# A hybrid decoder block on one core: causal masks added by VectorE, first MLP chunk in products of 512 columns, gate rows ahead of low parts

## What is computed

```python
h = rmsnorm(x, g_mix)
qa, ka, va, cq, ckv, kr, gate_a, gate_b = split(h @ w_in)
# path a: 8 heads of 64, rope on q and k; the one key block of 256 is the query's own, so plain causal attention
s = where(key <= query, q @ k.T * scale, -inf); o_a = softmax(s) @ v
# path b: q and k of 96 = 64 + 32 (rope), v of 64, from low-rank latents; same causal softmax
x = x + (sigmoid(gate_a + b0) * (o_a @ w_o_a) + sigmoid(gate_b + b1) * (o_b @ w_o_b)) @ w_out
u = relu(rmsnorm(x, g_mlp) @ w_ff1)              # 1024 x 4096
x = x + (u * u) @ w_ff2                          # 4096 x 1024
return rmsnorm(x, g_final)
```

## Time and profile before

| | |
|---|---|
| runs | 371.0 us median of 3 (370.7, 371.0, 373.78) |
| the profiled execution's own time | 371.31 us |
| its span, first to last instruction | 369.5 us |
| TensorE busy | 360.6 us, 98% of the span |
| VectorE busy | 281.1 us, 76% |
| ScalarE busy | 229.1 us, 62% |
| granted TensorE clock, mean | 0.99 |
| HBM | 75.44 MB read, 1.05 MB written |

### The profile page before, as it was taken

The page is one execution under the profiler, slowest core; times in us unless marked ns, Lnnn a source line. Parts: engine busy times, 40 slices in busy tenths (PEclk is TensorE's granted clock), DMA queues, the critical chain, the costliest instruction groups (busy, mean ns, idle before and its releaser), DMA issues.

```text
span 369.5 us, 5652 instructions
## 1 busy us (share of the span) xinstructions
PE 360.6 (98%) x2180; PEld 316.7 (86%) x2180; DVE 281.1 (76%) x379; ACT 229.1 (62%) x370; POOL 39.8 (11%) x61
## 2 busy tenths in 40 slices
PE   7999999999999999999999999999999999999993
PEld 6998889877778888888899899999999999999982
DVE  3677973964756757779387779997999899998584
ACT  5696435977576656145274657775877777666424
POOL 1232000000000010000120211101111111220002
PEclk8999999999999999999999999999999999999997
DMA  7999756773332364509346799989999999963003
GB/s 241 321 375 321 272 171 229 226 231 111 118 116 109 115 227 162 180 12 305 140 140 220 183 355 237 285 245 264 266 248 318 265 300 295 303 174 115 0 2 114
DMA packets 43430, 76.79 MB, mean 208 GB/s; under 512 B 1875, under 2 KB 21600, under 8 KB 43152
## 3 DMA queue, kind: packets, MB, share of 16 engines
q1 hardware_dynamic: 39072, 66.59, 53.0%
q0 software_dynamic: 4176, 9.64, 13.2%
q10 hardware_dynamic: 160, 0.27, 0.2%
HBM read 75.44 MB, written 1.05 MB: 207 GB/s over the span
## 4 chain that ended last, share of the span: by engine, by line
PE 96%; DMA 1%; DVE 0%; ACT 0%; POOL 0%; issue 0%; SPq 0%; POOLq 0%; ACTq 0%
PE ps L1345 29%; PE ps L1347 29%; PE ps L1346 29%; PE ps L1352 5%; PE ps L1484 2%; PE ps L1510 2%; DMA xs<-in_x_dram 1%; PE ps L1467 0%; POOL qkT_b L511 0%; PE ps L1423 0%; ACT qkT_b L524 0%; DVE xT_lo L1078 0%; DVE xs L1102 0%; ACT xT_hi L524 0%; POOLq L125 0%
## 5 line engine op out<-in xcount | busy, mean ns | idle before, releaser
L524 ACT ACTIVATE whi<-raw 128x1024 fp32r<-128x1024 f32 (+3 forms) x124 | 119.8, 1008 | 25.8 <-PE ps L1347 13.8
L889 DVE TENSOR_TENSOR wlo<-raw,whi 128x1024 fp32r<-128x1024 f32 (+3 forms) x68 | 73.9, 1119 | 29.2 <-ACT whi L524 28.7
L1345 PE MATMUL ps<-whi,xT_hi 128*128 128x512 f32 (+3 forms) x208 | 78.6, 378 | 0.3 <-DVE xT_lo L1078 0.3
L1347 PE MATMUL ps<-whi,xT_lo 128*128 128x512 f32 (+3 forms) x208 | 75.8, 365 | 0.0
L1346 PE MATMUL ps<-wlo,xT_hi 128*128 128x512 f32 (+3 forms) x208 | 75.8, 364 | 0.0
L1347 PE MATMUL ps<-xT_hi,wlo 128*128 128x256 f32 x224 | 63.4, 283 | 0.0
L1346 PE MATMUL ps<-xT_lo,whi 128*128 128x256 f32 x224 | 63.4, 283 | 0.0
L1345 PE MATMUL ps<-xT_hi,whi 128*128 128x256 f32 x224 | 63.3, 283 | 0.0
L1345 PE MATMUL ps<-whi,lat_hi 128*128 128x512 f32 (+2 forms) x134 | 51.7, 386 | 0.0
L1346 PE MATMUL ps<-wlo,lat_hi 128*128 128x512 f32 (+2 forms) x134 | 51.2, 382 | 0.0
L1347 PE MATMUL ps<-whi,lat_lo 128*128 128x512 f32 (+2 forms) x134 | 51.1, 382 | 0.0
(11 more groups left out here) (149 smaller groups left out, 479.9 us busy)
## 6 DMA issues: line engine op xcount, KB each, us to landing
raw<-in_w_ff_dram SPq DMA_DIRECT2D x32, 1024.0 KB, 7.8
raw<-in_w_in_dram SPq DMA_DIRECT2D x14, 1024.0 KB, 6.7
raw<-in_w_out_dram SPq DMA_DIRECT2D x4, 1024.0 KB, 5.1
t_raw<-in_w_ff_dram SPq DMA_DIRECT2D x12, 256.0 KB, 8.8
raw<-in_w_ff_dram POOLq DMA_DIRECT2D x12, 256.0 KB, 4.9
t_raw<-in_w_ff_dram POOLq DMA_DIRECT2D x12, 256.0 KB, 7.7
gates<-in_b_gate_dram POOLq DMA_DIRECT2D x2, 1024.0 KB, 6.5
raw<-in_w_o_a_dram SPq DMA_DIRECT2D x2, 1024.0 KB, 5.3
```

The lines of the kernel that those rows point to most:

```text
L524: return nc.scalar.activation(dst, src, ACT.Copy, scale=scale)
L889: nc.vector.tensor_tensor(wlo[:, s, h * w:(h + 1) * w], raw[:, s, h * w:(h + 1) * w], whi[:, s, h * w:(h + 1) * w].bitcast(F32), ALU.subtr ...
L1345: nc.tensor.matmul(dst, a_hi, b_hi, start=start, stop=False)
L1347: return nc.tensor.matmul(dst, a_lo, b_hi, start=False, stop=stop)
```

## The change

It has three parts.

1. The causal mask is added by VectorE. `masks` on TensorE is gone; the scores are written alone. A group is now the even or the odd heads, so a group is one bank. `row_max(g)` runs for each group: VectorE adds `causal` to the diagonal blocks in PSUM (L1009 of the new file, 512 elements per partition for t = 0 and 256 for t = 1), waits for that add (`masked`), and takes the maximum of that bank (L1011). The maximum of one bank is ready before the other's mask is added. On TensorE the scores of a pair now stand ahead of the values of the pair before, not behind them.
2. In chunk 0 of the MLP the two loads of w_ff1 hold 4 k-tiles of all 512 columns each, and `mlp_in_rows(t, k0, k1)` makes products of 512 columns. `turn_h(1)` stands after k-tile 6 of t = 0, `turn_u(0)` after k-tile 5 of t = 1.
3. On VectorE `gate_rows` stands ahead of `low_unit` after pairs 1, 3 and 5.

```diff
-GROUPS = [(path, t, range(h, h + (4 >> t))) for path in range(2) for t in range(TT)
-          for h in range(0, 8, 4 >> t)]
+GROUPS = [(path, t, range(h + odd, h + (8 >> t), 2)) for path in range(2) for t in range(TT)
+          for h in range(0, 8, 8 >> t) for odd in range(2)]
...
@@ SyncE
-                sp.dma_start(ff_slot(p).rearrange("p (k n) -> p k n", k=KT),
-                             w1_v[:, :, p * 256:(p + 1) * 256]).then_inc(raw_landed[(U_FF + p) % SLOTS], 16)
+                sp.dma_start(ff_slot(p).rearrange("p (k n) -> p k n", k=4),
+                             w1_v[:, 4 * p:4 * p + 4, 0:HALF]).then_inc(raw_landed[(U_FF + p) % SLOTS], 16)
...
@@ ScalarE, exps(g)
-                act.wait_ge(max_ready, g // 2 + 1)
+                act.wait_ge(max_ready, g + 1)
...
@@ VectorE
-            def row_max(pair):
-                heads = GROUPS[2 * pair][2]
-                n = len(heads)
-                top = negmax[:, 2 * pair:2 * pair + 2, 0:n]
-                dve.wait_ge(scored, pair + 1)
-                nc.vector.tensor_reduce(top.rearrange("p g (j b) -> p b (g j)", b=2) if n == 4 else
-                                        top.rearrange("p g b -> p b g"),
-                                        ps[:, S_BANK:S_BANK + 2, :].rearrange("p b (j k) -> p b j k", j=n),
-                                        AX_X, ALU.max, negate=True).then_inc(max_ready, 1)
+            def row_max(g):
+
+                path, t, heads = GROUPS[g]
+                keys, n = P * (t + 1), len(heads)
+                src = ps[:, S_BANK + g % 2, :].rearrange("p (h k) -> p h k", h=n)
+                diag = src[:, :, t * P:keys]
+                dve.wait_ge(scored, g // 2 + 1)
+                nc.vector.tensor_tensor(diag, diag, bcast(causal[:, :], n), ALU.add).then_inc(masked, 1)
+                dve.wait_ge(masked, g + 1)
+                nc.vector.tensor_reduce(negmax[:, g, 0:n], src, AX_X, ALU.max, negate=True).then_inc(max_ready, 1)
...
             for pair in range(PAIRS):
-                row_max(pair)
+                row_max(2 * pair)
+                row_max(2 * pair + 1)
...
-                low_unit(U_GATE + AHEAD + 1 + pair)
                 if pair % 2 == 1:
                     if pair == 1:
                         dve.wait_ge(bias_landed, 32)
                     gate_rows(pair // 2)
+                low_unit(U_GATE + AHEAD + 1 + pair)
...
@@ TensorE
-                if pair == 0:
-                    pe.wait_ge(qkT_ready, 11)
-                else:
-                    pe.wait_ge(pT_ready, 2 * pair)
-                n = HALF // keys
-                for b in range(2):
-                    dst = ps[:, S_BANK + b, :].rearrange("p (j k) -> p j k", j=n)[:, :, t * P:keys]
-                    nc.tensor.matmul(dst, ident_h[:, :], bcast(causal[:, :], n), start=True, stop=False,
-                                     skip_group_check=True)
...
                 if slot in SCORE_SLOT:
-                    masks(SCORE_SLOT.index(slot))
+                    scores(SCORE_SLOT.index(slot))
                 if slot in VALUE_SLOT:
-                    g = 2 * VALUE_SLOT.index(slot)
-                    values(g)
-                    values(g + 1)
-                if slot in SCORE_SLOT:
-                    scores(SCORE_SLOT.index(slot))
+                    values(VALUE_SLOT.index(slot))
...
+            def mlp_in_rows(t, k0, k1):
                 for k in range(k0, k1):
-                    w = slice(k * 256, (k + 1) * 256)
-                    m = product(ps[:, 4 + t, p * 256:(p + 1) * 256], xT_hi[:, k, t * P:(t + 1) * P],
-                                xT_lo[:, k, t * P:(t + 1) * P], whi[:, s, w], wlo[:, s, w], k == 0, k == KT - 1)
-                if p == 1 and k1 == KT:
+                    s, w = (U_FF + k // 4) % SLOTS, slice(k % 4 * HALF, (k % 4 + 1) * HALF)
+                    if t == 0 and k % 2 == 0:
+                        pe.wait_ge(wlo_ready, 2 * U_FF + k // 2 + 1)
+                    m = product(ps[:, 4 + t, :], xT_hi[:, k, t * P:(t + 1) * P], xT_lo[:, k, t * P:(t + 1) * P],
+                                whi[:, s, w], wlo[:, s, w], k == 0, k == KT - 1)
+                if k1 == KT:
                     m.then_inc(u_done, 1)
...
             pe.wait_ge(hT_lo, 2)
-            pe.wait_ge(wlo_ready, 2 * U_FF + 2)
-            mlp_in_rows(0, 0)
-            pe.wait_ge(wlo_ready, 2 * U_FF + 3)
-            mlp_in_rows(0, 1, 0, 4)
-            pe.wait_ge(wlo_ready, 2 * U_FF + 4)
-            mlp_in_rows(0, 1, 4, 6)
+            mlp_in_rows(0, 0, 6)
             turn_h(1)
-            mlp_in_rows(0, 1, 6)
+            mlp_in_rows(0, 6, KT)
             pe.wait_ge(hT_lo, 3)
-            mlp_in_rows(1, 0, 0, 4)
+            mlp_in_rows(1, 0, 4)
             pe.wait_ge(hT_lo, 4)
-            mlp_in_rows(1, 0, 4)
+            mlp_in_rows(1, 4, 5)
             turn_u(0)
-            mlp_in_rows(1, 1)
+            mlp_in_rows(1, 5, KT)
```

## The result

| | before | changed |
|---|---|---|
| median of this comparison | 370.85 us (370.19 to 373.78, 4 runs) | 367.28 us (366.97 to 367.49, 4 runs) |
| profiled execution's own time | 371.31 us | 367.49 us |
| its span | 369.5 us | 365.7 us |
| TensorE busy | 360.6 us | 357.1 us |
| VectorE busy | 281.1 us | 285.8 us |

The ratio is 0.9902, 95% interval 0.9877 to 0.9927: 3.6 us less. Two later comparisons of the same kernel gave 0.9922 (0.9899 to 0.9945) and 0.9899 (0.9871 to 0.9928). The first and the third lie at the 1% line, the second inside it.

The account below looks back on a forecast made before the run. TensorE, busy 360.6 of 369.5 us, was taken to bound the kernel. Masks -2.4, pair 0's wait +0.05 and chunk 0 -0.9 gave -3.2 us, so 367.9 us; 8 in 10 range 366.7 to 369.8.

Parts of the forecast that it names:

- TensorE sets the time, and what is taken off it comes out whole: Whole kernel: TensorE is busy 360.6 of 369.5 us, so work removed shortens it one for one unless a wait replaces it.
- Masks off TensorE, -2.4 us: Attention: six pairs' masks leave TensorE, 2 x 0.54 + 4 x 0.32 = 2.4 us saved.
- The low end of 1.7 us: Masks in attention: the saving if 0.11 us per pair for a change of operand kind stays, 1.7 us.
- Adds into PSUM, 0.69 and 0.42 us: VectorE's mask adds in attention: 0.69 us for 512 elements, 0.42 for 256, taken from the nearest rows.
- Pair 0 is tight and waits at most 0.05 us: Transposes of pair 0's second group: TensorE waits 0 to 0.05 us; 1.0 us at VectorE's upper price.
- Part 3, 0 by itself and cover for the adds: Gate rows first on VectorE: the next row maximum no longer queues behind them; cover for the adds, 0 by itself.
- Chunk 0, -0.9 us: MLP chunk 0: -0.6 us for columns, +0.15 before `turn_h(1)`, -0.43 for the old wait; 12.4 us instead of 13.3.
- the trace's 0.6 us: MLP chunk 0: 96 matmuls at 0.120 us become 48 at 0.227, 11.5 against 10.9, so 0.6 us less.
- the estimate of 0.1 us: MLP chunk 0: the skill page's spacing, 96 x 109 against 48 x 216 ns, would save only 0.1 us.
- The loop keeps the gain: MLP loop after chunk 0: transfers move with TensorE, so no new wait; closest call 1.76 us of slack.
- the case "more": Whole kernel: operand-kind changes cost the next instruction too, or small waits go; up to 1 us more, 366.8 to 367.3; 18%.
- the case "the other side": Attention: VectorE's add into PSUM far slower than any row; at 2.3 us per add the kernel takes 375.9 us; 4%.

Follow-up runs that it names:

- e8_values_first_add_twice: The changed kernel with values ahead of scores again and a second add, of zeros, behind each mask add; 372.68 us, run once.
- e10_masks_only_again: The changed kernel with MLP chunk 0 back in products of 256 columns, run a second time; 368.71 us, ratio 0.9912 to the kernel before.
- e2_masks_only: The changed kernel with MLP chunk 0 back in products of 256 columns, first time; 369.39 us, ratio 0.9954 to the kernel before.
- e9_changed_third: The changed kernel itself, with nothing altered, in its third comparison; 368.34 us, ratio 0.9899 to the kernel before.
- e11_zeros_at_end: The changed kernel with six bf16 matmuls of zeros behind its last product; 368.40 us, ratio 0.9913 to the kernel before.

## Why the prediction was right

The prediction was 367.9 us with 366.7 to 369.8, and 367.28 us was measured; 3.2 us less were forecast, 3.6 us measured, of which 2.7 us are shown behind the start. Point by point:

- **TensorE sets the time, and what is taken off it comes out whole.** Right: both stages' gains reached the end, each alone and together.
- **Masks off TensorE, -2.4 us.** The step that was mis-sized: 1.81 us. The start-to-start times of the earlier trace rows held 0.1 us for each pair that belongs to the half-array matmuls behind the mask. The row against it, showed full-array transposes following a product at ordinary pitch, and I read it as if it held for scores and values. The low end of 1.7 us was the better one: pure columns.
- **Adds into PSUM, 0.69 and 0.42 us.** Right to 0.01 us, and the order of the chain too:

```profile
80.75 0.69 DVE L1009 TENSOR_TENSOR ps<-ps,causal 128x512 f32<-128x512 f32 x1
81.47 0.69 DVE L1011 TENSOR_REDUCE negmax<-ps 128x4 f32<-128x512 f32 x1
...
89.77 0.42 DVE L1009 TENSOR_TENSOR ps<-ps,causal 128x256 f32<-128x256 f32 x1
```

- **Pair 0 is tight and waits at most 0.05 us.** Right. The transposes and the step to the next product take 0.80 us, as before:

```profile
85.92 1.03 PE L1354 MATMUL ps<-ident,prob 128*128 128x128 f32 x8
```

  With the adds doubled, 1.44 us more in the chain, it waited 1.2 us, and no other pair more than 0.13. So pair 0 has 0.25 us of slack, where the prediction had 0.05.
- **Part 3, 0 by itself and cover for the adds.** Right as cover, and its price is now known: 0.3 to 0.4 us. The 0 by itself was argued, not run.
- **Chunk 0, -0.9 us.** Right: 0.87. The 48 matmuls keep the pitch of 0.227 us, so the trace's 0.6 us was the right term for the columns and the estimate of 0.1 us from the Trainium skill (TensorE: Matmul & The Clock Gate, section Back-to-back issue gap) was not. The wait ahead of `turn_h(1)` is there, and the one behind it is gone:

```profile
190.54 0.39 PE L1349 MATMUL ps<-whi,xT_lo 128*128 128x512 f32 x1
190.92 1.09 PE L1354 MATMUL ps<-ident,rows 128*128 128x128 f32 x8
191.77 0.47 PE L1347 MATMUL ps<-whi,xT_hi 128*128 128x512 f32 x1
```

  The transposes start 0.38 us behind the last matmul instead of 0.23, a wait of 0.15 us, as forecast. The prediction counts 28 matmuls from the end of t = 0 to `turn_u(0)` before the change; there were 24, and nothing hung on it.
- **The loop keeps the gain.** Right. SyncE's first load of chunk 2 moved by 3.8 us, as much as the end of chunk 0 on TensorE, and the closest call has more slack than before, 230.31 to 232.64, 2.3 us against 1.76:

```profile
203.36 0.37 SPq L372 DMA_DIRECT2D raw<-in_w_ff_dram  x1
```

```profile
221.74 0.68 DVE L1152 TENSOR_TENSOR t_raw<-raw 128x512 f32<-128x512 f32 x1
...
229.22 1.09 DVE L1199 TENSOR_TENSOR lat_lo<-rows,lat_hi 128x896 fp32r<-128x896 f32 x1
```

```profile
232.64 0.40 PE L1347 MATMUL ps<-whi,lat_hi 128*128 128x512 f32 x1
```

  VectorE no longer waits for the transfer at that place.
- **The total.** It was closer than its terms, by luck. The masks gave 0.6 us less than forecast, and 0.9 us in the start that was no part of the forecast made up for it; with the stages alone the median would be 370.85 - 2.70 = 368.15 us. At 367.28 us the measurement lies at the lower edge of the forecast's 367.3 to 368.5, just inside the band of the case "more". That case gave a removed step of operand kind or other small waits as its reason, and neither happened: the step stayed. In the case "the other side", 375.9 us is reckoned from 371.31, the other cases from 371.0.

## What to carry over

Where one engine is busy from end to end and its instructions are pipelined, count a removed instruction by its own pitch in a run of its kind, not by the distance to the next instruction of another kind: the step between kinds stays behind and falls to the neighbour. Work moved to an engine with idle time is free only as far as the slack of each consumer goes; doubling that work once shows where it ends, and here it ended in the first pair alone. For differences under 1%, cut both traces at the same instructions, and at ones that the change leaves alone: stages of this kernel repeat to 0.04 us from one execution to another, a cut at the changed instructions hid 0.09 us, and the total moves by 1 to 2 us with its first 18.

## What the runs showed of the hardware

- Matmuls that each take a new stationary tile had a pitch of 0.227 us with 512 columns and 0.120 us with 256, at a granted clock of 1.00: 14 and 13 ns above the columns' own time at 2.4 GHz.
- Entering matmuls on half of the array cost about 0.1 us, whether a product, a mask or scores with 96 rows stood ahead (0.31 to 0.33 us behind a gate product, against 0.23 for full-array transposes and for scores with 96 rows). A bf16 matmul of 128 columns in the middle of such a row cost 0.36 us; in the middle of matmuls with 96 rows it cost 0.10 us.
- A VectorE add with input and output in the same PSUM bank took 0.69 us for 512 and 0.42 us for 256 elements, as much as adds of these sizes from PSUM to SBUF (0.69 us at 186.89 us of the changed kernel's trace, 0.42 in the earlier trace rows).
- The first 17 to 19 us, up to the CKV product, differed by up to 2.4 us between executions (16.8 us in `e8_values_first_add_twice`, 19.2 in `e10_masks_only_again`) with the same instructions: by when x landed (TensorE idle 0.7 to 1.9 us for it), and in five executions by a stretch at the first products, one to seven matmuls long, at 0.31 to 0.32 us of pitch instead of 0.17. 0.32 us is the time of 384 columns at 1.2 GHz. In the profiled execution of the kernel before the granted clock does read 0.50 there, from 8 to 10 us, after two idle times of 0.6 and 1.0 us; in the other four (`e2_masks_only`, `e9_changed_third`, `e10_masks_only_again`, `e11_zeros_at_end`) it reads 1.00 throughout. What stretched the pitch in those stays open.
